# A decoder block with 32 experts: another order of the expert weight loads, gate and up products in two banks, the last down product in three column pieces

## What is computed

```python
def reference(x, w_in, ..., ln1_g, ln1_b, w_router_group, w_router_expert, w_gate, w_up, w_down, ln2_g, ln2_b):
    alpha = (2.0 * DEPTH) ** 0.25
    for l in range(DEPTH):                                   # DEPTH = 1
        mix = hybrid_mixer(x, w_in[l], conv_w[l], w_out_conv[l], w_out_attn[l], w_o[l], slopes)
        x = layer_norm(alpha * x + mix, ln1_g[l], ln1_b[l])
        ffn = hierarchical_moe(x, w_router_group[l], w_router_expert[l], w_gate[l], w_up[l], w_down[l])
        x = layer_norm(alpha * x + ffn, ln2_g[l], ln2_b[l])
    return x

# in hierarchical_moe: one group of 4, in it two experts of 8 for each token; combine holds their weights
h = (silu(einsum('td,edf->tef', xt, w_gate)) * einsum('td,edf->tef', xt, w_up) * combine[..., None])
return einsum('tef,efd->td', h, w_down)
```

## Time and profile before

| | us |
|---|---|
| median of 3 runs (429.52, 431.32, 433.29) | 431.32 |
| the profiled execution | 430.34 |
| its span, first to last instruction | 428.4 |
| TensorE busy | 375.0 (88%) |
| VectorE busy | 166.1 (39%) |
| ScalarE busy | 132.0 (31%) |
| POOL busy | 29.5 (7%) |
| mean granted TensorE clock | 0.944 |
| loaded and stored | 132.69 MB, mean 310 GB/s |

### The profile page before, as it was taken

The page is one execution under the profiler, slowest core; times in us unless marked ns, Lnnn a source line. Parts: engine busy times, 40 slices in busy tenths (PEclk is TensorE's granted clock), DMA queues, the critical chain, the costliest instruction groups (busy, mean ns, idle before and its releaser), DMA issues.

```text
span 428.4 us, 7077 instructions
## 1 busy us (share of the span) xinstructions
PE 375.0 (88%) x2829; PEld 276.3 (65%) x2829; DVE 166.1 (39%) x330; ACT 132.0 (31%) x225; POOL 29.5 (7%) x40
## 2 busy tenths in 40 slices
PE   6899899999999999999899993793999796496694
PEld 6899898989899999999655452252355344144143
DVE  2544477777364646446712120055021202012026
ACT  3344454644444444418122121021030212011010
POOL 3000000000000000001000000285200000000004
PEclk9699999999999999999999998697799999599698
DMA  8799885736568686799489999998399999999912
GB/s 285 187 332 356 269 292 168 290 106 206 182 195 295 196 281 200 254 405 422 204 359 424 420 420 422 422 419 353 112 426 420 423 419 423 419 421 419 389 55 98
DMA packets 53998, 132.69 MB, mean 310 GB/s; under 512 B 6610, under 2 KB 39378, under 8 KB 42196
## 3 DMA queue, kind: packets, MB, share of 16 engines
q1 hardware_dynamic: 53908, 132.30, 80.7%
q0 software_dynamic: 64, 0.01, 0.0%
HBM read 131.25 MB, written 1.05 MB: 309 GB/s over the span
## 4 chain that ended last, share of the span: by engine, by line
PE 55%; DMA 25%; DVE 8%; SPq 5%; ACT 3%; issue 2%; POOL 1%; POOLq 0%; ACTq 0%; DVEq 0%
PE bank L1021 24%; DMA dn<-in_w_down 16%; PE bank L1253 7%; PE bank L1281 7%; DMA gu<-in_w_up 6%; PE bank L1139 5%; SPq L362 4%; PE bank L1116 3%; PE bank L1216 3%; DVE wl L722 2%; PE bank L1288 2%; DMA raw<-in_w_in 2%; ACT wh L572 1%; SPq L367 1%; PE bank L1184 1%
## 5 line engine op out<-in xcount | busy, mean ns | idle before, releaser
L722 DVE TENSOR_TENSOR wl<-raw,wh 128x1024 fp32r<-128x1024 f32 x56 | 68.4, 1224 | 70.2 <-ACT wh L572 69.9
L1021 PE MATMUL bank<-xh,wh 128*128 128x256 f32 x288 | 84.1, 292 | 3.5 <-DVE wl L722 3.5
L1021 PE MATMUL bank<-xl,wh 128*128 128x256 f32 x288 | 82.6, 287 | 0.0
L1021 PE MATMUL bank<-xh,wl 128*128 128x256 f32 x288 | 82.5, 286 | 0.0
L572 ACT ACTIVATE wh<-raw 128x1024 fp32r<-128x1024 f32 x56 | 58.7, 1055 | 63.4 <-PE bank L1021 36.6
L1253 PE MATMUL bank<-gu,xg 128*32 128x512 f32 (+1 forms) x576 | 60.5, 576 | 19.7 <-DMA gu<-in_w_up 19.7
L1021 PEld LDWEIGHTS bank<-xh,wh 128*128 128x128 f32 x288 | 56.4, 196 | 6.0 <-DVE wl L722 4.0
L1021 PEld LDWEIGHTS bank<-xl,wh 128*128 128x128 f32 x288 | 56.4, 196 | 0.2 <-issue 0.2
L1021 PEld LDWEIGHTS bank<-xh,wl 128*128 128x128 f32 x288 | 56.4, 196 | 0.0
L1253 PEld LDWEIGHTS bank<-gu,xg 128*32 128x32 f32 x576 | 18.5, 115 | 56.6 <-issue 53.4
L1281 PE MATMUL bank<-dn,hT 128*32 128x512 f32 x232 | 33.5, 678 | 12.7 <-DMA dn<-in_w_down 12.7
(11 more groups left out here) (197 smaller groups left out, 460.9 us busy)
## 6 DMA issues: line engine op xcount, KB each, us to landing
gu<-in_w_gate SPq DMA_DIRECT2D x32, 1024.0 KB, 14.2
gu<-in_w_up SPq DMA_DIRECT2D x32, 1024.0 KB, 23.0
dn<-in_w_down SPq DMA_DIRECT2D x25, 1024.0 KB, 18.5
raw<-in_w_in SPq DMA_DIRECT2D x40, 512.0 KB, 4.7
raw<-in_w_o SPq DMA_DIRECT2D x8, 512.0 KB, 4.6
dn<-in_w_down SPq DMA_DIRECT2D x8, 512.0 KB, 15.9
raw<-in_w_out_conv SPq DMA_DIRECT2D x4, 512.0 KB, 3.6
raw<-in_w_out_attn SPq DMA_DIRECT2D x4, 512.0 KB, 4.5
```

The lines of the kernel that those rows point to most:

```text
L722: dve.tensor_tensor(wl[:, s, :].rearrange("p (k c) -> p k c", k=KC), raw[:, pair % NRAW, :].rearrange("p (k c) -> p k c", k=KC) [:, :, n % ...
L1021: mm = pe.matmul(dst, w[:, k, :], v[:, i, :], start=(i == 0 and w is h and v is high_in), stop=(i == len(ks) - 1 and w is l))
```

## The change

- Loads: quad 3's four up loads move from before quad 2's last down load to behind it and the two rows of normalisation weights; quad 3's down loads stand ahead of quad 4's gate and up loads, where they had stood behind.
- Gate and up products are separate in every quad, gate into bank 6 and up into bank 5, with 256 columns each; the sigmoid waits for the gate product only.
- The down product and the scatter have three pieces (`Y_PIECES`): columns 0 to 511, 512 to 767 and 768 to 1023, in banks 4, 5 and 6. `y_ps` counts three pieces per round, and `y_taken` has a semaphore for each. In the last quad the first piece's scatter stands ahead of the third piece's product, and the down matrices are loaded in the three pieces, twelve loads instead of eight.
- The last quad's gate and up loads have a semaphore each; TensorE waits for them one by one, and behind each of the first three up waits it does four small products.
- The seed moves from behind quad 4 to behind quad 6. POOL's `x1n` waits for a count of `y_ps`.
- `shift` is one operation; the statistics of the second normalisation wait for pieces.

The diff, cut to its core:

```diff
+Y_PIECES = ((4, 0, HALF), (5, HALF, HALF + HALF // 2), (6, HALF + HALF // 2, DM))
+NY = len(Y_PIECES)
+WARM_LAST = 4
...
+            def load_last_gu(c):
+
+                for e in range(QE):
+                    sp.dma_start(gu[(NQ - 1) % 2][:, e, c, :, :],
+                                 (wg_v, wu_v)[c][:, (NQ - 1) * QE + e, :, :]).then_inc(last_gu_in[c][e], 16)
...
             sp.wait_ge(gu_ps, through(2))
-            load_gu(1, 3)
-            sp.wait_ge(y_ps, 2 * through(2))
+            load_gu(1, 3, parts=[0])
+            sp.wait_ge(y_ps, NY * through(2))
             for e in range(NE_EARLY, QE):
                 load_dn_one(2, e)
             for i, v in enumerate((ln1_g, ln1_b)):
                 sp.dma_start(ln_row[0:1, i, :], v[0:1, :]).then_inc(ln_in, 16)
-
+            load_gu(1, 3, parts=[1])
+            sp.wait_ge(y_ps, NY * through(3))
+            load_dn(3)
             for q in range(4, NQ - 1):
                 sp.wait_ge(gu_ps, through(q - 1))
                 load_gu(q % 2, q)
-                if q == 4:
-                    sp.wait_ge(y_ps, 2 * through(3))
-                    load_dn(3)
-                sp.wait_ge(y_ps, 2 * through(q))
+                sp.wait_ge(y_ps, NY * through(q))
                 load_dn(q)
             sp.wait_ge(gu_ps, through(NQ - 2))
-            load_gu((NQ - 1) % 2, NQ - 1)
-            sp.wait_ge(y_ps, 2 * through(NQ - 1))
-            for h in range(2):
-                load_dn_cols(h, NQ - 1)
+            for c in range(2):
+                load_last_gu(c)
+            sp.wait_ge(y_ps, NY * through(NQ - 1))
+            for i in range(NY):
+                load_dn_cols(i, NQ - 1)
...
+            pool.wait_ge(rounds_done, 1)
+            pool.wait_ge(y_ps, 2 * pool.value_load(bounds[0:1, 4:5], min_val=1, max_val=MAX_ROUNDS))
             for t in range(TT):
                 into = x1n[:, t, :].rearrange("q (p k) -> q k p", k=KC)
...
-            link(pool.tensor_tensor(shift[:, 0:1], moments[:, t, 0:1], rstd[:, t:t + 1], ALU.mult))
-            pool.tensor_scalar(shift[:, 0:1], shift[:, 0:1], -1.0, None,
-                               ALU.mult).then_inc(shift_done, 1)
+            pool.tensor_scalar(shift[:, 0:1], moments[:, t, 0:1], rstd[:, t:t + 1], -1.0,
+                               ALU.mult, ALU.mult).then_inc(shift_done, 1)
...
-                act.wait_ge(gu_ps, n)
+                act.wait_ge(gate_ps, n)
                 act.activation(sg[:, :], bank[6][:, 0:DE], ACT.Sigmoid).then_inc(sg_done, 1)
...
-            dve.wait_ge(added, 4 * total + 2)
+            first = 2 * TT + TT * NY * last
             for t in range(TT):
+                dve.wait_ge(added, first + t + 1)
                 dve.bn_stats(stats[:, t, 0, :], bank[2 * t][:, :])
             for t in range(TT):
-                dve.wait_ge(added, 4 * total + 3 + t)
+                dve.wait_ge(added, first + TT * (NY - 1) + t + 1)
                 link(dve.bn_stats(stats[:, t, 1, :], bank[2 * t + 1][:, :]))
...
-                        pe.wait_ge(gu_in[half], 2 * QE * 16 * loads)
-                        passes = [slice(0, 1), slice(1, 2)] if q == 0 else [slice(0, 2)]
-                        for part in passes:
+                        if not last_quad:
+                            pe.wait_ge(gu_in[half], 2 * QE * 16 * loads)
+                        for part in range(2):
+                            if last_quad:
+                                pe.wait_ge(bank_free[7], c + 1)
+                                for e in range(QE):
+                                    pe.wait_ge(last_gu_in[part][e], 16)
+                                    if part and e < QE - 1:
+                                        stay_warm(WARM_LAST)
...
+                        down(0)
+                        down(1)
+                        if last_quad:
+                            scatter(0)
+                            down(2)
+                        else:
+                            down(2)
+                            scatter(0)
+                        scatter(1)
+                        scatter(2)
                         gather(c + 1)
...
-                if q == 4:
+                if q == NQ - 2:
                     pe.wait_ge(x1_done, X1_PARTS)
                     seed(True)
```

63 lines of the change are left out of this document (34 added, 29 removed).

## The result

| | before | changed |
|---|---|---|
| median, us | 431.10 (4 runs, 429.52 to 433.29) | 419.40 (4 runs, 417.78 to 419.62) |
| ratio, with its 95% interval | | 0.972 (0.967 to 0.977) |
| the profiled execution, us | 430.34 | 417.78 |
| its span, us | 428.4 | 415.7 |
| TensorE busy, us | 375.0 (88%) | 374.1 (90%) |

The change takes 11.7 us off the median, 2.7%. 417.8 had been forecast, with 413.5 to 422.0 around it.

The account below looks back on a forecast made before the run. One FIFO of loads was taken to bound the expert half. Scatter end 418.69 to 405.85 plus 0.15 made 13.0 us off 430.34, 417.3; half of a 1.0 median offset gave 417.8 us, range 413.5 to 422.0.

Parts of the forecast that it names:

- The cause of the hole: Load queue near 300 us: quad 3's down loads issued late; reordering loads brings every later landing 9.15 us earlier.
- POOL in the way of VectorE in quad 3: Quad 3: POOL's large operations stretch VectorE's slot masks and delay the quad by 3.5 us.
- The first rival: Near 268 us: quad 2's down product comes late; half a hole gives about 422, a whole one about 427; chance 0.10.
- POOL's new wait: POOL's second-residual work waits for the eighth down piece, in quad 2's down product; claimed cost nothing, 80 us of cover.
- Quad 6 and the seed: Quad 6's product at 360.7, seed until 386.4, gate product until 389.95, up product at 392.6.
- Twice the instructions cost nothing: Gate and up in two passes: 7.11 us against 7.07 in one, so no cost.
- The last loads hide: Last quad's twelve down loads: last piece lands at 400.5 plus 0.4 at most, wanted at 403.1, hidden by 2 us.
- Small products, clock, product times: Last quad: small products take 2.65 us together, TensorE runs at the full 2.4 GHz, up product from 392.6 to 396.15.
- Product to down product: Up product's end to down product's start: 2.5 us; a round shrinks by 0.15 us at most, taken as 0.
- Behind the scatter: After the last scatter: later statistics +0.14, POOL's shift as one operation -0.29, together -0.15 us.
- The fourth: Rival: the twelve small last loads run one by one; end of scatter 425, 435 us, slower than before; chance 0.02.
- The third: Rival: clock falls in quad 5 or 6, 14 instead of 8.8 us in quad 6 at most; 419 to 422; chance 0.13.

Follow-up runs that it names:

- b_order: The kernel before with the new load order alone (quad 3's up and down loads moved): median 421.09 us, ratio 0.982.
- a_warm0: The changed kernel without the twelve small products between the last up waits: median 418.47 us, ratio 0.976.
- a_seed4: The changed kernel with the seed behind quad 4 again, small products kept: median 418.30 us, ratio 0.976.
- a_best: The changed kernel without the twelve small products and with the shift in two operations: median 417.43 us, ratio 0.969.

## Why the prediction was right, and where its steps were not

**The cause of the hole: right, and its size nearly.** 9.15 us were forecast "on every later landing". In b_order, the order alone, quad 6 begins 10.0 us earlier and the last product 8.6; the 9.14 in E lies this close to the forecast by luck, as said there. That each step was right can be read from the issues: quad 3's down loads at 264.5 forecast, 262.83 + 1.38 (X was 1.38 earlier) = 264.2 measured; quad 4's at 288, and 287.52 + 1.38 = 288.9. The queue never ran dry: the ten windows of 5 us from 250 to 300 us all have a share of 1.00 or more. The first rival, a hole that moves, did not come.

**POOL in the way of VectorE in quad 3: right in kind.** 3.5 us of delay were allowed; the transposes waited 2.75 and the clock fell after it (granted 0.71 from 280 to 285), so that the down product took 5.31 instead of 3.65: 4.4 together. The timeline of VectorE and, last, of POOL:

```profile
273.05 4.00 DVE L972 TENSOR_SCALAR rank<-rank  x1
277.29 2.90 DVE L923 TENSOR_TENSOR pick<-slot_id,rank 128x128 f32<-128x128 f32 x2 [0.24 <-DVE rank L972]
```

```profile
269.88 2.90 POOL L548 TENSOR_TENSOR x1n<-x1p,lng 128x1024 f32<-128x1024 f32 x1 [9.68 <-issue]
```

POOL's new wait, on the eighth down piece, cost nothing that the trace shows: its work began 9.68 us after its last broadcast, with nothing in the profile that it waited for, and before the change it had stood 8.34 us in the same place. It began with quad 3's product, 7 us behind the down product that it waits for. The 10 us of cover that the queue was said to have behind quad 3 held too.

**Quad 6 and the seed: 0.7 us too early, by two errors that nearly cancel.** From X the forecast had quad 6 at 150.1, the gate product at 175.8 and the up product at 182.0; measured were 150.83, 176.23 and 182.70. The step that failed here is "Twice the instructions cost nothing". It was right on TensorE (7.11 us against 7.07, again), and wrong in the queue, where the instruction packets of the second passes made landings 1.5 us later. The forecast was only 0.7 off, as quad 6 without that delay would have begun at 149.3, 0.8 earlier than the 150.1 that I had put down: I had taken off 9.15 where quad 6 gained 10.0. That the two errors offset each other is luck.

**The last loads hide: right, with a margin half as wide.** The forecast was that TensorE is last by 2 us. The edits that took TensorE's work away won 1.24 and 1.07 us and then met loads, so the margin is some 1.2 us. Three things were off. The last up load landed at 180.5 from X, where 390.3, or 179.7, had been forecast. The last down piece landed 10.95 us behind it instead of 10.6, since the 384 GB/s taken for 1 KB rows are not theirs: in the window of the earlier trace rows from which they were read, half the bytes came in rows of 8 KB, as the view of DMA traffic for 20 to 30 us shows (1888 packets of at most 1 KB make 1.9 of the 3.84 MB):

```profile
DMA packets 2130, 3.84 MB, mean 384 GB/s; under 512 B 82, under 2 KB 1888, under 8 KB 1888
```

A window of the changed kernel in which nearly all packets are under 2 KB has less, at a full share:

```profile
394.00:396.00 2.00, 2.00 (x37) 1.19 (x26) 0.33 (x1) 0.06 (x1) 0.00 (x0) 1.00 1.10 352
```

And the load that TensorE meets first is not the last piece, as the forecast had it, but the second: the waits of a_warm0, a_seed4 and a_best stand in front of its product. The rule of the Trainium skill that was set against the forecast (DMA: Bandwidth & Descriptors, Rules for kernel authors, 1 MiB per DMA) is true in its direction here, since smaller loads moved less per us. But the price of about 2.0 us for each load in a row, which its section on the anatomy of one DMA gives for DMAs issued from GpSimd, did not come for these, which SyncE issues. In a_warm0 the first eight of the twelve landed by 398.01, 8.2 us after the last up load.

**Small products, clock, product times: right.** 2.65 forecast and 2.88 measured; the up product ran in 3.66 us, at the full 2.4 GHz, which is granted from 366 us on (0.50 still at 360 to 362, after 8.21 us of idling):

```profile
360.00:362.00 2.00, 1.99 (x20) 1.00 (x24) 0.00 (x0) 0.00 (x0) 0.00 (x0) 0.50 1.00 414
...
366.00:368.00 2.00, 2.00 (x44) 1.11 (x39) 0.42 (x1) 0.09 (x1) 0.00 (x0) 1.00 1.03 430
```

What had not been foreseen is that they are of no use: the pause they fill is 0.7 us, and the clock stays up without them.

**Product to down product: 0.4 us better than taken.** The round was taken not to shrink, "0.15 at most". It went from 2.5 to 2.1 us (395.5 to 397.63), as the sigmoid and the first multiplication now lie under the up product and TensorE no longer waits for `hs`. The four pieces of down product and scatter took 7.63 us instead of 7.2, which takes that back.

**Behind the scatter: the sign was wrong.** −0.15 was forecast and +0.73 measured. The step that failed is "POOL's shift is one operation instead of two ... −0.29". The operation did get 0.3 us shorter and ScalarE did start earlier. But I had followed only the chain of who waits for whom, and had not asked which engine would run beside which after the shift: POOL's product moved in front of VectorE's second operation and slowed it by 1 us, the third store waited for VectorE, and the last two stores left together, 0.2 us later and 0.4 us longer on their way.

**The sum.** From X the forecast was 217.84 − 13.0 = 204.8, and 206.52 was measured, 1.7 more: 0.8 at the scatter's end and 0.9 behind it. The profiled execution came out at 417.78 against 417.3 only because its first stage was 1.4 us faster than that of the kernel before. The medians, 419.40 and 417.90, are 1.6 and 0.1 us above the forecast.

Two sums among the rivals are off. The fourth, with the scatter's end at 425, gives 430.34 + 425 − 418.69 = 436.7 us and not 435. The third's 14 us instead of 8.8 give 417.8 + 5.2 = 423, above the 422.0 at which the range ends. Neither rival came.

## What to carry to other kernels

When one FIFO of loads bounds a stretch, add up the idle share of its queue over the windows: that sum, 9.15 us, came back as 8.6 to 10.0 us in the landings when the order was mended, and the place to mend is the load that waits in front of others for a buffer whose reader waits for a load behind it. Once such a hole is closed the end of the kernel decides, and there gains of 1 us are found by asking for each wait which of the two, engine or load, comes last, and whether work put into a wait is longer than the wait. Shortening a small operation on the path can cost more than it saves, if it shifts a large operation of POOL in front of one of VectorE; look at what runs beside what, not only at what waits for what. And when a queue never runs dry, a load lands with the engine that is furthest behind: a kernel with more instructions can pay for them there.

## What the runs showed of the hardware

- VectorE and POOL slow each other down at the end of this kernel, and the one that begins second pays: VectorE's second 128x512 operation took 1.76 us behind POOL's start and about 0.7 ahead of it, POOL's product 1.26 and 1.66. This held in all 14 profiles of the study, by a difference of 0.3 us in POOL's start.
- A full queue had different rates by the form of its loads: 418 to 424 GB/s with the 1 MB loads, 387 with the 512 KB loads of 2 KB rows, 352 with the 256 KB loads of 1 KB rows. Size and row length changed together, so the two are not told apart.
- Products split in two passes cost nothing on TensorE (7.11 against 7.07 us), but their instructions are fetched through the same engines as the loads, in packets of 16 KB and about 1.1 us. By the times of the 16 parts of a load, each packet left one part 1.5 us late until the queue was next dry: 2, 4, 7, 8 and 11 packets, and as many delays, in five kernels.
- TensorE's clock was granted at full from 366 us to the last scatter, with and without the twelve small products; after the pauses of 3.16 to 10.66 us in this study that lowered it the next product took 8.46 to 9.89 us instead of 7.1.
